# Four units of seven block products per layer of a SwiGLU feed-forward, one behind the other, in place of three

## What is computed

```python
mix = ...                                   # the mixer of this layer
h = h + mix
hn = rms_norm(h, norm_ffn_g[layer])
h = h + (jax.nn.silu(hn @ ffn_w_gate[layer]) * (hn @ ffn_w_up[layer])) @ ffn_w_down[layer]
```

## Time and profile before

| | us |
|---|---|
| median of 3 runs | 559.45 (559.22 to 559.7) |
| the profiled execution, its own time | 559.39 |
| its span, first to last instruction | 557.6 |

### The profile page before, as it was taken

How to read it: one execution, slowest core, us unless ns; L and a number is a source line. 1 busy time by engine, 2 the same in 40 slices (tenths; PEclk the granted TensorE clock), 3 DMA queues, 4 the chain that set the end, 5 groups by cost and what they waited for, 6 DMA issues and landing times.

```text
span 557.6 us, 7496 instructions
## 1 busy us (share of the span) xinstructions
PE 551.2 (99%) x2877; PEld 468.8 (84%) x2877; DVE 467.6 (84%) x562; ACT 341.3 (61%) x471; POOL 20.4 (4%) x60
## 2 busy tenths in 40 slices
PE   9999999999999999999999999999999999999996
PEld 8899988888888888888888888888888888888885
DVE  5779996788996997997798998977889889979875
ACT  6778664756664773666566366647387557656724
POOL 1200001000000000000000000000000000000000
PEclk9999999999999999999999999999999999999999
DMA  8995544474379259277469422444916790773502
GB/s 300 409 401 199 185 150 152 150 216 163 121 277 336 97 182 343 78 285 290 148 253 366 168 75 76 156 147 158 306 64 224 287 320 21 222 286 143 197 1 75
DMA packets 31429, 111.95 MB, mean 201 GB/s; under 512 B 3489, under 2 KB 4641, under 8 KB 30625
## 3 DMA queue, kind: packets, MB, share of 16 engines
q1 hardware_dynamic: 30384, 105.04, 50.2%
q0 software_dynamic: 864, 6.29, 5.8%
q10 hardware_dynamic: 144, 0.14, 0.1%
HBM read 110.40 MB, written 1.05 MB: 200 GB/s over the span
## 4 chain that ended last, share of the span: by engine, by line
PE 99%; DVE 0%; DVEq 0%; issue 0%; ACT 0%; ACTq 0%
PE bank L1834 16%; PE bank L1832 16%; PE bank L1833 16%; PE bank L2277 8%; PE bank L2324 7%; PE bank L2328 7%; PE bank L2323 7%; PE bank L2282 4%; PE bank L1943 4%; PE bank L1946 2%; PE bank L1896 1%; PE bank L1893 1%; PE bank L1889 1%; PE bank L1915 1%; PE bank L2289 1%; PE bank L2035 1%
## 5 line engine op out<-in xcount | busy, mean ns | idle before, releaser
L1120 DVE TENSOR_TENSOR w_lo<-raw,w_hi 128x2048 fp32r<-128x2048 f32 (+2 forms) x98 | 217.2, 2232 | 18.2 <-ACT w_hi L632 16.7
L632 ACT ACTIVATE w_hi<-raw 128x2048 fp32r<-128x2048 f32 (+2 forms) x81 | 149.5, 1861 | 11.4 <-PE bank L1834 7.4
L1832 PE MATMUL bank<-w_lo,yT_hi 128*128 128x512 f32 (+1 forms) x242 | 96.5, 399 | 0.0
L1834 PE MATMUL bank<-w_hi,yT_lo 128*128 128x512 f32 (+1 forms) x242 | 94.1, 389 | 0.0
L1833 PE MATMUL bank<-w_hi,yT_hi 128*128 128x512 f32 (+1 forms) x242 | 94.0, 388 | 0.0
L1834 PEld LDWEIGHTS bank<-w_hi,yT_lo 128*128 128x128 f32 x242 | 45.4, 188 | 9.6
L1832 PEld LDWEIGHTS bank<-w_lo,yT_hi 128*128 128x128 f32 x242 | 45.5, 188 | 8.4 <-DVE yT_lo L1335 0.2
L1833 PEld LDWEIGHTS bank<-w_hi,yT_hi 128*128 128x128 f32 x242 | 45.6, 188 | 8.2
L2277 PE MATMUL bank<-xT,w_hi 128*128 128x512 f32 x192 | 48.5, 394 | 0.0
L949 ACT ACTIVATE w_hi<-raw 128x2048 fp32r<-128x2048 f32 x24 | 45.8, 1910 | 2.9 <-DMA raw<-in_slabs 2.6
L1832 PE MATMUL bank<-w_lo,xT 128*128 128x512 f32 (+1 forms) x112 | 42.8, 382 | 0.0
(11 more groups left out here) (247 smaller groups left out, 973.3 us busy)
## 6 DMA issues: line engine op xcount, KB each, us to landing
raw<-in_slabs SPq DMA_DIRECT2D x170, 512.0 KB, 4.8
spare<-in_slabs SPq DMA_DIRECT2D x16, 512.0 KB, 7.0
raw<-in_slabs POOLq DMA_DIRECT2D x6, 1024.0 KB, 9.7
raw<-in_slabs SPq DMA_DIRECT2D x5, 256.0 KB, 4.3
h<-in_x SPq DMA_DIRECT2D x2, 512.0 KB, 7.1
early<-in_norm_ffn_g SPq DMA_DIRECT2D x2, 512.0 KB, 10.1
raw<-in_slabs SPq DMA_DIRECT2D x6, 128.0 KB, 4.6
h<-in_x_cols SPq DMA_DIRECT2D x1, 512.0 KB, 5.5
```

Of the source, the lines that this page charges most:

```text
L632: A(w_hi[:, s % SLOTS, c], raw_of(r, c), ACT.Copy).then_inc(hi_ready, 1)
L1120: V.tensor_tensor(w_lo[:, s % SLOTS, c], raw_of(preps[s][0], c), w_hi[:, s % SLOTS, c].bitcast(F32), ALU.subtract).then_inc(lo_ready, 1)
L1832: T.matmul(o, st_hi, mv_lo, start=first, stop=False, skip_group_check=onto)
L1834: return T.matmul(o, st_lo, mv_hi, start=False, stop=last, skip_group_check=onto)
```

## The change

Units now stand at chunks 2, 4, 6 and 8 of each layer; chunks 2 and 5 are no longer plain, only chunk 10 is. For a unit behind another (4, 6, 8) the two halves of the earlier `down` product are taken apart, one between `t2` and `t1` and one behind `t1`; in unit 2 the halves of `down` of chunk 1 stand behind `b11`, `t2` and `t1`. `b22` comes ahead of `b21`, and the own `down` halves stand behind `b21` and behind `t4`, the third `turn` in the middle of the last. The banks of a unit's second sum alternate between 6 and 5. `make_forms` and the split of its result move ahead of the fourth transposed quarter of chunks 0 and 1. `block_add` 0 of the next unit stands between `seven_act_lo` 1 and `seven_gate` 2. For unit 8 the fourth weight sum is made by a second adding DMA (`add_fourth`). At the end of layer 0 two turns stand inside the first pair of chunk 10. `used_no` counts released slots in the new order. The first split of the next layer's slabs moves behind the norm's scale. The core of the diff:

```diff
-SEVEN_AT = ((3, 6, 8), (3, 6, 8))
-WHOLE = [("block", l, a + 1, 1) for l in range(2) for a in SEVEN_AT[l]]
+SEVEN_AT = ((2, 4, 6, 8), (2, 4, 6, 8))
+ADDED = ((8,), (8,))
...
+                prepare(("down", l, before(l, i)), d, d_made)
+                free(d)
                 prepare(("t3", l, i), y, None)
                 prepare(("t2", l, i), x, None)
-                prepare(("down", l, before(l, i)), d, d_made)
-                free(d)
                 e, e_made = load(("block", l, i, 1))
                 place["raw", l, i] = ((x, x_made), (y, y_made), (z, z_made), (e, e_made))
                 prepare(("t1", l, i), y, None)
                 free(y)
                 d, d_made = load(("down", l, i + 1))
-                prepare(("b21", l, i), e, e_made)
                 prepare(("b22", l, i), z, z_made)
                 free(z)
-                free(e, ("sum", 3 * units + 3))
+                prepare(("b21", l, i), e, e_made)
+                free(e, *[("sum", sums_no(l, i + 1))][:i not in ADDED[l]])
+                prepare(("down", l, i + 1), d, d_made)
+                free(d)
                 prepare(("t4", l, i), x, None)
                 free(x)
-                prepare(("down", l, i + 1), d, d_made)
-                free(d)
...
+            return (6, 5)[(SEVEN_AT[l].index(a) + k) % 2]
...
+            def add_fourth(l, a):
+                x, _ = place["raw", l, a][0]
+                n = [key for key, _, _ in loads].index(("block", l, a, 1))
+                pool.wait_ge(lo_ready, place["t2", l, a] + 1)
+                pool.wait_ge(*sum_made(l, a, 1))
+                nc.gpsimd.dma_start(raw_of(x), piece(n, 0, SLAB), accum_op=ALU.add).then_inc(fourth_added, 16)
             for n, (kind, a, b) in enumerate(POWS):
...
                 silu(0, 1, 0)
-                split_his(f + 6, f + 7)
+                split_his(f + 6)
                 at_hi_evac(1, 1, 1, 0)
+                act.wait_ge(forms_made, l + 1)
+                A(forms_hi[:, :, :, :], forms[:, :, :, :], ACT.Copy).then_inc(forms_hi_ready, 1)
                 silu(1, 1, 1)
                 at_hi_evac(2, 0, 0, 1)
-                at_hi_evac(3, 1, 1, 1)
...
+                    follows, leads = a - 2 in SEVEN_AT[l], a + 2 in SEVEN_AT[l]
+                    seven_copy(a, 0)
+                    if not follows:
                         next_hi()
+                    else:
                         seven_hi(a - 2, 3)
+                    next_hi()
+                    seven_copy(a, 1)
+                    next_hi(2)
+                    seven_copy(a, 2)
+                    seven_silu(a, 0)
+                    next_hi(2)
+                    seven_hi(a, 0)
+                    seven_silu(a, 1)
+                    next_hi()
+                    seven_hi(a, 1)
+                    seven_silu(a, 2)
+                    next_hi()
+                    if leads or l:
                         seven_hi(a, 2)
                     seven_silu(a, 3)
                     next_hi()
+                    if leads:
                         next_hi()
+                        return
+                    if l == 0:
+                        seven_hi(a, 2)
+                    seven_hi(a, 3)
+                next_hi()
+                at_hi_evac(3, 1, 1, 1)
+                for a in SEVEN_AT[l]:
+                    seven(a)
...
+                make_forms()
                 activate(2, 0)
-                split_los(f + 6, f + 7)
+                split_los(f + 6)
                 at_lo_evac(1, 1, 1, 0)
                 activate(3, 1)
+                dve.wait_ge(forms_hi_ready, l + 1)
+                V.tensor_tensor(forms_lo[:, :, :, :], forms[:, :, :, :], forms_hi[:, :, :, :].bitcast(F32),
+                                ALU.subtract).then_inc(forms_ready, 1)
                 at_lo_evac(2, 0, 0, 1)
-                make_forms()
-                at_lo_evac(3, 1, 1, 1)
...
                 def seven(a):
                     follows, leads = a - 2 in SEVEN_AT[l], a + 2 in SEVEN_AT[l]
+                    block_add(a, 1)
+                    if a not in ADDED[l]:
+                        block_add(a, 2)
                     next_lo()
                     if follows:
                         seven_act_lo(a - 2, 3)
+                    next_lo()
+                    seven_add(a, 0)
+                    next_lo()
+                    seven_gate(a, 0)
+                    next_lo()
+                    seven_act_lo(a, 0)
+                    next_lo()
+                    seven_gate(a, 1)
                     seven_add(a, 1)
+                    next_lo()
                     seven_act_lo(a, 1)
                     if leads:
                         block_add(a + 2, 0)
+                    seven_gate(a, 2)
                     seven_add(a, 2)
+                    next_lo()
+                    seven_gate(a, 3)
                     if leads:
                         next_lo()
+                        seven_act_lo(a, 2)
                         next_lo()
                         return
+                    seven_act_lo(a, 2)
+                    if l:
                         next_lo()
                     seven_act_lo(a, 3)
+                block_add(SEVEN_AT[l][0], 0)
+                next_lo()
+                at_lo_evac(3, 1, 1, 1)
+                next_lo()
+                for a in SEVEN_AT[l]:
+                    seven(a)
...
                     pe.wait_ge(act_ready, U + 2 * a + j + 1)
+                    if j and not (j == 3 and a == SEVEN_AT[l][-1]):
+                        pe.wait_ge(at_lo, U + 2 * a + j)
                     for k in range(2):
                         last = T.transpose(turned(l, a, j)[:, k * P:(k + 1) * P], seven_out[j][:, k * P:(k + 1) * P],
...
+                    below = dict(half=0, ip=half_of_acts(l, d), release=True)
+                    if follows:
                         pe.wait_ge(act_ready, U + 2 * a - 2)
                         product("b11", a, 4, *a11)
+                        pe.wait_ge(seven_added, added - 1)
+                        product("t3", a, u, *s3)
+                        pe.wait_ge(seven_copied, copied + 1)
+                        product("t2", a, 4, *s2, midway=lambda: turn(d, 3), onto=True)
+                        down(d, 2 * a - 2, down_slab(l, d), **above)
+                        pe.wait_ge(seven_copied, copied + 2)
+                        product("t1", a, 4, *s1, onto=True)
+                        down(d, 2 * a - 1, down_slab(l, d), **below)
+                    else:
+                        pe.wait_ge(act_ready, U + 2 * a - 1)
+                        product("b11", a, 4, *a11)
+                        down(d, 2 * a - 3, down_slab(l, d), half=0, ip=half_of_acts(l, d))
+                        pe.wait_ge(forms_ready, l + 1)
+                        product("t3", a, u, *s3)
+                        pe.wait_ge(seven_copied, copied + 1)
+                        product("t2", a, 4, *s2, onto=True)
+                        down(d, 2 * a - 1, down_slab(l, d), half=1, ip=half_of_acts(l, d), blocks=(0,))
+                        pe.wait_ge(seven_copied, copied + 2)
+                        product("t1", a, 4, *s1, onto=True)
+                        down(d, 2 * a - 1, down_slab(l, d), half=1, ip=half_of_acts(l, d), blocks=(1,))
                     pe.wait_ge(seven_copied, copied + 3)
                     product("b22", a, 4, *s4, onto=True)
+                    if follows:
+                        pe.wait_ge(seven_added, added)
+                    product("b21", a, w, *a12, midway=lambda: turn(a, 0))
+                    down(b, 2 * a, down_slab(l, b), 0, half_of_acts(l, b))
                     pe.wait_ge(seven_added, added + 1)
+                    product("t4", a, u, *a22, midway=lambda: turn(a, 1), onto=True)
+                    if l or b < e - 1:
+                        down(b, 2 * a + 1, down_slab(l, b), 1, half_of_acts(l, b), between=lambda: turn(a, 2))
+                for a in SEVEN_AT[l]:
+                    seven(a)
...
                 d, used = before(l, e), up_done if l == 0 else slab_used
-                if not ends_mixed(l, d):
-                    pe.wait_ge(act_ready, U + 2 * e - 2)
-                    pair(up_slab(l, e), up_slab(l, e), 4, used, last_turn(d))
+                def last_turns():
+                    if l == 0:
+                        turn(d, 2)
+                    turn(d, 3)
+                pe.wait_ge(act_ready, U + 2 * e - 2)
```

More of the change, by code:

```diff
@@ L78, in half_of_acts, with sums_no @@
     return (i + sum(i - 2 >= a for a in SEVEN_AT[l])) % 2
+def sums_no(l, i):
+    return sum(3 - (a in ADDED[m]) for m in range(l + 1) for a in SEVEN_AT[m] if m < l or a < i)
 def places():
@@ L204, in seven_no, with used_no @@
         return len(SEVEN_AT[0]) * l + SEVEN_AT[l].index(i)
-    def ends_mixed(l, a):
-        return l == 0 and a == NCH - 3
+    def used_no(s):
+        return used.get(s, s + 1)
+    used = {}
+    for l in range(2):
+        for a in SEVEN_AT[l]:
```

(30 more changed lines are left out.)

216 lines of the change are left out of this document (27 added, 189 removed).

## The result

| | before | after |
|---|---|---|
| median of 4 runs each, us | 559.34 (559.14 to 559.70) | 565.14 (564.89 to 565.44) |
| ratio, 95% interval | | 1.0103 (1.0086 to 1.0121) |
| profiled execution: time, span, us | 559.39, 557.6 | 565.0, 563.0 |

The account below looks back on a forecast made before the run. TensorE bounds the kernel (99% of the span), with VectorE left little room. New waits of 4.92 us in layer 0 and 4.30 in layer 1, together 9.22, less 4.50 saved: 4.7 us slower, 564.2 us, range 560.3 to 567.0.

Parts of the forecast that it names:

- TensorE's work: Each layer loses two plain chunks (33.20 us) and gains one unit (30.95 us): 2.25 us less, 4.50 in both.
- (a): Start of feed-forward: make_forms moved ahead and the forms' low part delay at_lo_evac 2, chunk 0's second down half: 0.83 us.
- (b): Unit 2, T being the end of its b11: VectorE starts split f+8 late, TensorE waits 1.71 us at the third turn.
- (c): Units 4 and 6: waits of 0.59 us at the third turn and 0.29 at t1's low split, 0.88 us a unit.
- the handover to TensorE: From the start of a small VectorE result to TensorE's matmul: 0.67 us, with 0.45 and 0.9 as ends.
- (d): End of layer 0 only: the last turn, inside chunk 10's first pair, waits for VectorE after unit 8, 0.62 us.
- The moved norm split: Split moved behind the norm's scale: costed at nothing, covered by three down halves and more; without cover 2.2 us.
- Loads: add_third of unit 2 lands 9.7 us after issue, plain loads take 4.8 us: 2 us and more to spare.
- the cover holds: Rival: VectorE runs ahead at these places and nothing of the waits remains, 555.0 us, chance 0.10.
- Half of it: Rival: the ties of (c) and (d) resolve, only (a) and (b) remain, 560.0 us, chance 0.10.
- a slab operation's spacing of 2.20 us: VectorE's start-to-start cost; the rival took the whole length of 2.29 us instead, about 568 us, chance 0.02.
- loads did not take over: Rival: unit 4's b11 slab lands 0.2 to 3 us late in each layer, up to 570 us, chance 0.08.

Follow-up runs that it names:

- e8: Changed kernel, VectorE's slab additions cut to 256 of 2048 columns (result wrong), orders of e2 and e3, norm's low part behind one split: 558.50 us, ratio 0.9978.
- e3: Changed kernel with at_lo_evac 2 ahead of the low part of the forms: 563.19 us, ratio 1.0067.
- e2: Changed kernel with ScalarE's hi part of slab f+8 (t2 of unit 2) ahead of seven_copy 0: 562.96 us, ratio 1.0061.
- e1: Changed kernel with block_add 0 of the next unit moved from ahead of gate 2 to behind the third seven_add: 568.25 us, ratio 1.0155.
- e5: Changed kernel with block_add 0 of the next unit between gate 2 and the third seven_add: 564.60 us, ratio 1.0084.
- e9: Changed kernel with the sum for t4 by an adding DMA in every unit, orders of e2, e3 and e5: 571.61 us, ratio 1.0211.
- e10: As e9, but block_add 0 of the next unit stays ahead of gate 2, as in the changed kernel: 575.07 us, ratio 1.0279.
- e12: Changed kernel with the edits of e2 and e3 together: 562.12 us, ratio 1.0042.
- e11: Changed kernel with the sum for t4 as a GpSimd tensor_tensor in units 2, 4 and 6, orders of e2, e3 and e5: 574.03 us, ratio 1.0251.
- e7: As e9, plus the addition for t1 ahead of the split of t2 and the norm's low part behind one split: 571.99 us, ratio 1.0236.
- e4: Changed kernel with the split of slab nxt put back ahead of the norm's addition and scale, end of layer 0: 571.78 us, ratio 1.0215.

## Why the prediction was right, point by point

- **TensorE's work, -4.50 us: right.** e8 has units of 31.0 us against 33.20 for two plain chunks, 2.2 us a layer.
- **VectorE as the limit from unit 2 to unit 8: right, and shown.** With its slab additions short (e8) every wait from unit 2 up to the last turn of unit 8 is gone. In the changed kernel the window from third turn to third turn has VectorE busy for all but 0.5 us (length, then busy PE, PEld, DVE):

```profile
160.95:192.62 31.67, 31.43 (x140) 25.31 (x140) 31.17 (x24) 20.77 (x20) 0.87 (x1) 1.00 0.72 232
192.62:224.27 31.65, 31.41 (x141) 25.32 (x141) 31.16 (x24) 20.76 (x20) 0.89 (x1) 1.00 0.74 232
```

  The forecast had 31.1 us of work for it and 31.8 for the unit.
- **(a) 0.83 us: measured 0.79** (e3).
- **(b) 1.71 us: measured 28.24 - 26.38 = 1.86**, the second number from e8. Put at one place, the third turn, it stands at two, `t1` (0.97: first turn at T + 18.20 against 17.23) and the third turn (0.89). The first comes from the gap ahead of f+8; the second stays when the gap is nearly closed (e2). In layer 1 it is 27.88 - 26.38 = 1.50 (T at 411.22, third turn at 439.10), with less at `t1`.
- **(c) 0.88 us a unit: measured 0.69** (31.67 against 30.98). The way from first to third turn is 9.56 us instead of 9.72, and from the third to the next first turn 0.28 us are lost as forecast (0.29). As two separate waits they were a wrong picture: e1 and e5 show one queue in which the loss only moves. The term that was too large is the handover to TensorE, taken as 0.67 us with 0.45 as its lower end. Gate 2 of unit 4 and the turn behind it, VectorE and then TensorE of the changed kernel, start 0.47 us apart:

```profile
192.15 0.42 DVE L1661 TENSOR_TENSOR work<-early,work 128x256 f32<-128x256 f32 x1
...
192.62 0.44 PE L2233 MATMUL bank<-ident,work 128*128 128x128 f32 x2 [0.24 <-DVE work L1661]
```

  It is as much in unit 2 (160.95 - 160.48), where VectorE reaches gate 2 at T + 27.77 and not T + 27.4.
- **(d) 0.62 us: measured about 0.5.** The first turn of unit 8 to the layer's last turn is 257.51 - 246.17 = 11.34 us (forecast 11.44, TensorE ready at 10.82). It stays in e8; no run removed it.
- **The moved norm split, costed at nothing: wrong.** The step looked at TensorE's queue (three halves of `down`) and not at VectorE's, where the norm's low part now stands behind two splits. VectorE's rows at that place, changed kernel:

```profile
274.42 1.41 DVE L1205 SCALAR_TENSOR_TENSOR early<-h,rstd,early 128x512 f32<-128x512 f32 x2 [0.68 <-POOL rstd L650]
276.57 4.50 DVE L1120 TENSOR_TENSOR w_lo<-raw,w_hi 128x2048 fp32r<-128x2048 f32 x2 [0.74 <-ACT w_hi L669]
280.98 1.28 DVE L1240 TENSOR_TENSOR xT<-bank,xT 128x512 fp32r<-128x512 f32 x2
```

  TensorE lost 1.20 - 0.23 = 0.97 us. The bound that I had given, 2.2 us without cover, held.
- **Loads: right.** Between units 2 and 8 no wait of TensorE or VectorE ends with a DMA. The spare's loads landed faster than the 7.0 us of the earlier trace rows (page of the changed kernel, part 6, KB each and median us to landing):

```profile
spare<-in_slabs SPq DMA_DIRECT2D x20, 512.0 KB, 4.2
```

- **The sum.** Layer 0: 0.79 + 1.86 + 1.38 + 0.5 + 0.97 = 5.5 us; layer 1: 0.79 + 1.50 + 1.38 = 3.7. Together 9.2, less 4.4: 4.8 us of the 5.4 between the two spans. The forecast's 4.7 lacked the 0.97 and had 0.4 us too much in each layer's (c). 0.6 us between the spans, and 1.0 of the 5.8 between the medians, are not located.
- **The rivals.** Of "the cover holds" the mechanism is shown by e8, its condition did not hold. "Half of it" fell with (c) and (d) standing, a slab operation's spacing of 2.20 us held (the row of two splits is 4.50 us long, 2.20 more than one of 2.29), and loads did not take over until e9 and e10 added more of them.

No run beat the kernel before with all its work done. The nearest, e12, is 0.4% behind; what it lacks is VectorE time (2.19 us a layer).

## What to carry to other kernels

When TensorE bounds a kernel at 99% and another engine is busy for 90% of the same stretch, a change that trades TensorE's work for the other's has to be costed in the other's queue, operation by operation, and ahead of every step that TensorE needs. Once that queue is full, moving an operation within it mostly moves the wait (e5), while closing a gap in it does bring time (e2, e3). Taking an operation away helps only where it isn't already hidden behind a handover (here an addition done while ScalarE made the hi part of the next slab). Of a step that a change moves, ask first whether its buffer is free at the old place.

## What was not expected of the hardware

- An elementwise addition of 128x2048 float32 takes GpSimd 4.6 to 4.9 us. A split on VectorE beside it ended 2.17 us after it and took 4.97 us in place of 2.29 (e11, unit 4).
- A second adding DMA of 1 MB was issued on GpSimd's queue only 8.2 to 9.7 us after the first (starts 136.48 and 146.17 in e7, 171.17 and 179.49 in e9), with no semaphore named as the cause, and the data of the second was there 11.8 us after its issue, against a median of 9.2. What holds the second back was not separated.
- Waits of TensorE up to 1.2 us left the granted clock at its full level (0.999 over the changed kernel). Behind some of the longer ones it fell to 0.50, the lower of its two levels (1.2 of 2.4 GHz), and such a wait cost more than its own length. The length of the wait alone doesn't decide it: in e11, whose waits of 2.41 us in unit 4 and 2.42 us in unit 6 stand at the same place, it fell behind the first and stayed at 1.00 behind the second, and the same again in layer 1 (2.40 and 2.41 us). In unit 4 three matmuls in a row then start 0.42 and 0.43 us apart, where 0.23 is usual, until the clock is back at about 180.4 (TensorE's timeline of e11, then a window behind each of the two waits):

```profile
176.64 1.87 PE L2264 MATMUL bank<-w_lo,forms_hi 128*128 128x512 f32 x4 [2.41 <-DVE w_lo L1134]
178.31 0.63 PE L1788 MATMUL bank<-w_lo,yT_hi 128*128 128x512 f32 x1
178.73 0.63 PE L1789 MATMUL bank<-w_hi,yT_hi 128*128 128x512 f32 x1
179.16 0.63 PE L1790 MATMUL bank<-w_hi,yT_lo 128*128 128x512 f32 x1
...
212.23 1.20 PE L2264 MATMUL bank<-w_lo,forms_hi 128*128 128x512 f32 x4 [2.42 <-DVE w_lo L1134]
...
177.00:179.00 2.00, 2.00 (x6) 1.58 (x5) 2.00 (x1) 0.46 (x1) 0.00 (x0) 0.50 0.65 219
213.00:215.00 2.00, 2.00 (x10) 1.64 (x9) 2.00 (x2) 0.60 (x1) 0.00 (x0) 1.00 0.89 283
```

  It fell too in e9 (0.70 in the window 233 to 238, behind a wait of 2.24 us) and in e10 (0.50 from 228 to 232, behind a wait of 4.03 us), but not behind the waits of 2.19 and 2.24 us in units 2 and 4 of e10 (1.00 from 160 to 168 and from 193 to 200). What sets the one apart from the other is not shown. So the times of e4 and e9 to e11 are no measure of the waits alone.
- A float32 operation on VectorE of 2048 columns that is as long as 2.29 us comes every 2.20 us in a row, in the changed kernel as before.
